# A two-part fp32 block on one core: rounded matmuls that take their 256 moving columns in turns of 16, and moving inputs 128 bytes behind the weights

## What is computed

```
def swiglu_layer(x, norm_g, w_gate_up, w_down):
    h = rmsnorm(x, norm_g)
    g, u = jnp.split(h @ w_gate_up, 2, axis=-1)
    return x + (jax.nn.silu(g) * u) @ w_down
```

## Time and profile before

| | |
|---|---|
| median of 3 runs | 1959.55 us (1958.71 to 1959.64) |
| the profiled execution | 1960.96 us |
| its span, first to last instruction | 1959.2 us |
| TensorE matmuls | 1880.1 us busy (96%), 18191 instructions |
| VectorE | 1340.3 us busy (68%) |
| ScalarE | 747.2 us busy (38%) |
| granted TensorE clock, mean | 0.99 of 2.4 GHz |

### The profile page before, as it was taken

How to read it: one execution, slowest core, us unless ns; L and a number is a source line. 1 busy time by engine, 2 the same in 40 slices (tenths; PEclk the granted TensorE clock), 3 DMA queues, 4 the chain that set the end, 5 groups by cost and what they waited for, 6 DMA issues and landing times.

```text
span 1959.2 us, 42020 instructions
## 1 busy us (share of the span) xinstructions
PE 1880.1 (96%) x18191; PEld 1745.0 (89%) x18191; DVE 1340.3 (68%) x1755; ACT 747.2 (38%) x1099; POOL 88.6 (5%) x131
## 2 busy tenths in 40 slices
PE   8999999999899999999999999998999999999999
PEld 7987999998699999998887899997998887889988
DVE  8896678658648866864676469666764766458755
ACT  5572533434533332222234334254213233325154
POOL 2000000000400000002000000000002000000000
PEclk9999999999999998999999999998999999999999
DMA  8554477864347785653540145554662542035644
GB/s 220 142 151 144 134 262 256 262 188 137 100 130 258 250 255 121 171 162 98 150 130 25 46 111 166 145 151 118 163 183 79 154 131 59 25 99 162 167 117 137
DMA packets 473225, 291.90 MB, mean 149 GB/s; under 512 B 26775, under 2 KB 467580, under 8 KB 472872
## 3 DMA queue, kind: packets, MB, share of 16 engines
q1 hardware_dynamic: 466720, 262.13, 47.7%
q0 software_dynamic: 5312, 25.32, 3.4%
q10 hardware_dynamic: 1032, 2.11, 0.4%
HBM read 287.95 MB, written 1.05 MB: 148 GB/s over the span
## 4 chain that ended last, share of the span: by engine, by line
PE 79%; DVE 12%; ACT 4%; issue 2%; DMA 1%; POOL 0%; ACTq 0%; DVEq 0%; SPq 0%
PE bank L709 39%; PE bank L1488 6%; PE bank L1487 6%; PE bank L1489 5%; DVE rounded L734 3%; PE bank L698 3%; PE bank L668 3%; PE bank L950 2%; PE bank L1693 1%; PE bank L1680 1%; ACT rounded L723 1%; DVE rounded L718 1%; PE bank L1117 1%; PE bank L942 1%; PE bank L1661 1%
## 5 line engine op out<-in xcount | busy, mean ns | idle before, releaser
L709 PE MATMUL bank<-rounded 128*128 128x256 f32 (+1 forms) x5160 | 622.7, 281 | 11.0 <-DVE rounded L734 8.7
L709 PEld LDWEIGHTS bank<-rounded 128*128 128x128 f32 (+1 forms) x5160 | 607.8, 186 | 21.2 <-DVE rounded L734 12.8
L734 DVE TENSOR_TENSOR rounded<-arena,rounded 128x1024 fp32r<-128x1024 f32 (+1 forms) x275 | 331.9, 1214 | 76.8 <-ACT rounded L723 69.3
L1487 PE MATMUL bank<-parts 128*128 128x256 f32 x1024 | 288.0, 281 | 1.8 <-DVE parts L2314 1.6
L1489 PE MATMUL bank<-parts 128*128 128x256 f32 x1024 | 289.1, 282 | 0.0
L1488 PE MATMUL bank<-parts 128*128 128x256 f32 x1024 | 287.7, 281 | 0.0
L774 ACT ACTIVATE arena<-bank 128x512 f32<-128x512 f32 x114 | 67.7, 597 | 352.2 <-PE bank L709 338.9
L709 PE MATMUL bank<-common,arena 128*128 128x256 f32 x896 | 199.4, 380 | 0.0
L1487 PEld LDWEIGHTS bank<-parts 128*128 128x128 f32 x1024 | 195.2, 191 | 2.8 <-issue 1.4
L723 ACT ACTIVATE rounded<-arena 128x1024 fp32r<-128x1024 f32 x144 | 150.5, 1056 | 115.1 <-PE bank L709 73.1
L1488 PEld LDWEIGHTS bank<-parts 128*128 128x128 f32 x1024 | 193.7, 189 | 0.1
(11 more groups left out here) (409 smaller groups left out, 2407.7 us busy)
## 6 DMA issues: line engine op xcount, KB each, us to landing
arena<-in_w_in SPq DMA_DIRECT2D x190, 512.0 KB, 3.8
whole<-in_ffn_w_gate_up SPq DMA_DIRECT2D x44, 1024.0 KB, 5.2
arena<-in_ada_w POOLq DMA_DIRECT2D x32, 768.0 KB, 6.5
whole<-in_ffn_w_down SPq DMA_DIRECT2D x16, 1408.0 KB, 7.2
arena<-in_rec_w_in SPq DMA_DIRECT2D x36, 512.0 KB, 3.9
arena<-in_att_w_qkv SPq DMA_DIRECT2D x24, 512.0 KB, 3.9
arena<-in_rec_w_out SPq DMA_DIRECT2D x16, 512.0 KB, 4.0
arena<-in_mla_w_o SPq DMA_DIRECT2D x16, 512.0 KB, 4.1
```

What stands on the lines that cost most here:

```text
L709: last = pe.matmul(psum[s][0:c, m % 2 * T:m % 2 * T + T], w[a][:, k, cols], x[b][:, k, :], start=(k, a, b) == (0, 0, 0), stop=k == job.kt ...
L734: dve.tensor_tensor(raw_view(job_of[u], u, UNIT_LOW), raw, high_view(job_of[u], u).bitcast(F32), ALU.subtract)\
L1487: pe.matmul(bank, w_hi, x_hi, start=start and k == 0, stop=False)
```

## The change

Two edits, and no instruction is added, removed or moved on any engine. First, in every rounded matmul with 256 moving columns the moving operand and the PSUM output are both read and written in another order: 16 numbers from the first 128, 16 from the second 128, the next 16 of the first, and so on. Each of the 256 results lands where it did. Native matmuls (`order` is the identity for them) stay as they are. Second, the three shift constants become 32 numbers (128 bytes) for high and low parts alike.

```
-        X_SHIFT, H_SHIFT, HIDDEN_SHIFT = (16, 16), (16, 32), (64, 64)
+        X_SHIFT, H_SHIFT, HIDDEN_SHIFT = (32, 32), (32, 32), (32, 32)
...
+        def alternating(x):
+
+            return x.rearrange("p (a l j) -> p l a j", a=2, j=16)
...
+            order = alternating if job.high else lambda v: v
...
-                                last = pe.matmul(psum[s][:, t * COLS:t * COLS + COLS], x[b][:, at + k, t * P:t * P + P],
-                                                 w[a][:, k, n * COLS:n * COLS + COLS], start=begins, stop=ends, skip_group_check=True)
+                                last = pe.matmul(alternating(psum[s][:, t * COLS:t * COLS + COLS]), x[b][:, at + k, t * P:t * P + P],
+                                                 alternating(w[a][:, k, n * COLS:n * COLS + COLS]), start=begins, stop=ends, skip_group_check=True)
...
-                            last = pe.matmul(psum[s][0:c, m % 2 * T:m % 2 * T + T], w[a][:, k, cols], x[b][:, k, :],
+                            last = pe.matmul(order(psum[s][0:c, m % 2 * T:m % 2 * T + T]), w[a][:, k, cols], order(x[b][:, k, :]),
                                              start=(k, a, b) == (0, 0, 0), stop=k == job.kt - 1 and (a, b) == passes[-1])
...
-                x_hi, x_lo = (e[:, k, :] for e in x)
+                x_hi, x_lo = (alternating(e[:, k, :]) for e in x)
...
-                    last = three_passes(psum[s][:, m * T:m * T + T], UP_W[s], slice(m * P, m * P + P), DK, H_PARTS, True, True)
+                    last = three_passes(alternating(psum[s][:, m * T:m * T + T]), UP_W[s], slice(m * P, m * P + P), DK, H_PARTS, True, True)
```

More of the change, by code:

```diff
@@ L667, in first_units_by_pieces @@
                         for kk in (k, k + 1):
-                            last = pe.matmul(psum[s][:, i * T:i * T + T], w[a][:, kk, :], job.rhs[b][:, kk, :],
+                            last = pe.matmul(alternating(psum[s][:, i * T:i * T + T]), w[a][:, kk, :], alternating(job.rhs[b][:, kk, :]),
                                              start=(i, kk, a, b) == (0, 0, 0, 0), stop=kk == job.kt - 1 and a == 1, skip_group_check=True)
@@ L1501, in ffn_pe @@
                         for kk in (k, k + 1):
-                            last = pe.matmul(psum[0][:, m * T:m * T + T], UP_W[0][a][:, kk, m * P:m * P + P], H_PARTS[b][:, kk, :],
+                            last = pe.matmul(alternating(psum[0][:, m * T:m * T + T]), UP_W[0][a][:, kk, m * P:m * P + P], alternating(H_PARTS[b][:, kk, :]),
                                              start=(m, kk, a, b) == (0, 0, 0, 0), stop=kk == DK - 1 and a == 1, skip_group_check=True)
@@ L1526, in ffn_pe @@
                     pe.wait_ge(lo_ready[0].sem, j * 2 + (turns + UPS + q + 1))
-                    three_passes(psum[q][:, 0:T], DOWN_W[0], slice(0, P), UPS, [x[:, 0:UPS] for x in HIDDEN_PARTS], True, False)\
+                    three_passes(alternating(psum[q][:, 0:T]), DOWN_W[0], slice(0, P), UPS, [x[:, 0:UPS] for x in HIDDEN_PARTS], True, False)\
                         .then_inc(first_part_used.sem, 1)
@@ L1530, in ffn_pe @@
                     pe.wait_ge(lo_ready[1].sem, j * 2 + (turns + UPS + q + 1))
-                    three_passes(psum[q][:, 0:T], DOWN_W[1], slice(0, P), UPS, [x[:, UPS:] for x in HIDDEN_PARTS], False, True)\
+                    three_passes(alternating(psum[q][:, 0:T]), DOWN_W[1], slice(0, P), UPS, [x[:, UPS:] for x in HIDDEN_PARTS], False, True)\
                         .then_inc(product[q].sem, 1)
```

## The result

The change makes the kernel slower by 14 us: a median of 1973.34 us (1972.88 to 1977.63, 4 runs) against 1959.6 us (1958.71 to 1960.34, 4 runs) of the kernel before on the same chip. The ratio is 1.0075, with a 95% interval of 1.0057 to 1.0093. The profiled execution of the kernel after took 1973.37 us, with a span of 1971.6 us.

A forecast was written before the change was run, and what follows sets the result against it. TensorE bounds the kernel. Savings of 9.3 (gate and up), 7.2 (down) and 24.6 us (rest) give 34.7 us at the end, less 0.7 for VectorE: 34 us off 1960.96, a median of about 1926 us, range 1888 to 1964.

The forecast's parts named there:

- What bounds the kernel: Whole kernel: TensorE is busy 96% of the span and holds 79% of the chain, so its pace shows nearly in full.
- the place sets the pace: Rounded matmuls: one shape has at least three paces, 113.4 to 120.2 ns, differing with the place of the operands.
- the pace after: All 9768 rounded 256-column matmuls: 113.4 ns each after the change, bounded from below by 109.2 ns.
- Overtaking: Rounded matmuls: the moving read overtakes the weights' read modulo 512 bytes once or twice per matmul, which costs; the change removes it.
- the floor: Rounded matmuls: a floor near 113 ns, from 24 matmuls with 16 weight columns at 114 ns each.
- The slower rival: All rounded matmuls: 15 jumps between halves cost one tick each, 119.7 ns, 20 us more on TensorE, 1977 us; chance 0.14.
- The argument against it: L1661 reads two runs of 64 at 118 ns, L1680 one at 67 ns; so a read jump costs nothing that shows.
- Lower floor: All rounded matmuls: 109.2 ns, 4.2 ns more saved each, 59 us in the end, 1900 us; chance 0.26.
- The shift alone: Shift constants: cost nothing elsewhere, since VectorE and ScalarE write the inputs in the same number of instructions.
- Give-back: VectorE, 95% busy from 24 to 60 us and 92% from 1175 to 1216 us: 0.7 us taken off the saving.

The follow-up runs named there:

- e4: Kernel before with its old column order and all three shift constants at (48,48): 1944.75 us, ratio 0.9941.
- e1: Kernel before with the new column order but the old shift constants: 1978.02 us, ratio 1.0097.
- e3: Not the network: stretches of 96 rounded matmuls varying shift, turns and start; 113.5 ns consecutive at 48, 120.1 ns in turns of 16 at 32.
- e5: Changed kernel, new column order kept, with all three shift constants at (48,48): 1972.02 us, ratio 1.0080.
- e9: Not the network: matmul stretches varying columns, weight columns and turn lengths, plus native ones; turns of 16 with 16 weight columns took 120.2 ns.
- e11: Not the network: matmul stretches at each place from four beginnings; two halves in turns of 16 gave 120.0 ns at 0, 16, 32 and 48.
- e10: e4 with the other moving inputs (MLA latents, GLA inputs, M_HIGH, DIRECT_HIGH) also at distance 48: 1942.91 us, ratio 0.9937.

## Why the prediction was wrong

- **What bounds the kernel** held. TensorE's pace shows in the end: 23 us of pace gave 12.4 us of span, less by idle time and clock that can be named.
- **That the place sets the pace** held, in outline. It is the distance between the two operands, modulo 256 bytes and not 512 as I had it. With consecutive columns at 48, e4 brings TensorE half of the saving that I had expected of the change.
- **The step that failed is "the pace after".** I took 113.4 ns from the idea that two reads at one pace never overtake. With the turns both reads do run at nearly one pace in address (120.0 / 128 = 0.94 ns a number, against the 0.85 that I had estimated for the weights), yet rounded matmuls take 120.0 ns or a little more at every shift tried (e1, e3, e5, e9, e11), with 16 weight columns too (e9), where there is hardly a weight read to meet. Overtaking is thus not what costs there. With consecutive columns the distance of the two reads matters (0 costs with 128 weight columns and not with 16), but that they cost by overtaking was not singled out, and paces of 116.7 to 120.0 ns with 16 weight columns speak against it as the only cause. The one row on which I rested the floor, 24 matmuls with 16 weight columns at 114 ns, was one of these several paces. (By its own figures the prediction's 107 ns for 128 weight columns is 108.6; nothing hangs on it.) The error is 6.6 ns x 9768 = 64 us of TensorE time, and the sign follows from it: 41 us saved were forecast, 23 us more came.
- **The slower rival was right in place and size**: 119.7 ns and 1977 us against 120.0 and 1973, and "a pace of one value above 117.6 ns everywhere, whatever the shift". Its unit was not: it charged each of the 15 jumps one tick. Turns of 16 from four quarters have as many jumps and ran at 113.3 in two stretches (e9, e11).
- **The argument against it was the weak place.** It read the price of a jump off L1661, a native product. A native record takes 215.8 ns for 256 columns, twice as long, and a native matmul leaves two of them (e9), so what the prediction calls a native matmul is half of one. L1661 also has a single jump, between runs of 64. e9 shows that native matmuls run equally fast in both orders, so no native row could have shown this cost. I had given the rival 0.14 on that evidence.
- **Lower floor**: no stretch of 256 columns with 128 weight columns went below 113.3, nor with 16. That rival is out for all places and orders tried.
- **The shift alone** was costed at nothing elsewhere, rightly, but 32 is a poor distance: 118.7 ns, and 0.2% slower by itself.
- **Give-back.** The prediction took 0.7 us for VectorE coming late. In e4, with half of the saving, VectorE holds 17% of the chain, and the wait for L734 grows from 9.6 to 12.4 us, but all idle time of TensorE grows by 1.9 us only. The term was small rightly; it was not what failed.

Still open: why two halves in turns of 16 never take less than 18 ticks for 16 columns while four quarters can, and what picks 113.3 or 117.8 at one distance from one stretch to the next. The beginning matters (e11), by a rule that these runs don't show, and equal beginnings did not give equal paces in different programs. A cure that pins the start of each stretch was not tried.

## What to carry to other kernels

Where TensorE bounds the kernel with rounded (fp32r) matmuls, read the pace, the distance of starts, and not the durations, and try the distance between moving and stationary operand modulo 256 bytes: here 48 numbers against 16 to 64 gave 0.6% for three constants, while a distance of 0 holds the slowest pace of consecutive columns, 120.0 ns. Leave the moving columns consecutive unless a test in the same type says otherwise: a cheap-looking access pattern costed from fp32 matmuls says nothing on fp32r ones. A few hundred matmuls in stretches, each different in one thing, would have told this before the change was made.

## What was not expected of the hardware

- Rounded matmuls of one shape mostly take one of a few paces, 113.3, 117.8, 118.7 or 120.0 ns for 256 columns at distances in steps of 16 numbers, and the same code at the same addresses can run at two of them (e4 and e10).
- Turns of 16 between two halves take 288 ticks for 256 columns, where consecutive columns take 272 at best, and the read alone brings this about; turns of 8 took 123.4 ns and of 4 129.5 ns (124.4 with 16 weight columns). Native matmuls pay nothing for turns of 16.
- A PSUM output in runs of 64 bytes cost nothing in the two stretches that had it alone.
- A native matmul leaves two records in the trace: the 96 written for L192 appear as x192, 215.8 ns apart, so that one of 256 columns takes 432 ns against 113 to 120 of a rounded one.
